# Reordering around TensorE in a hybrid decoder layer: early key and query turns, split head transposes, a later shared expert, and seven half products for the last gate

## What is computed

```
xn  = rms_norm(h);  proj = xn @ w_in
gdn: q,k,v = silu(causal_conv(proj)); q,k = l2_norm; 8 heads of the chunked gated delta rule -> o_a
     y_a = (rms_norm(o_a) * silu(z)) @ w_branch_gdn
fox: q,k = rms_norm per head (16 heads of 64), causal softmax attention with log-forget decay -> y_f
h   = h + (sigmoid(m_a) * y_a + sigmoid(m_f) * y_f) @ w_out
t   = rms_norm(h);  scores = sigmoid(t @ w_router);  top 8 of 64 experts, weights normalised * 2.5
h   = h + sum_e gate_e * (silu(t @ we_gate_e) * (t @ we_up_e)) @ we_down_e + shared expert (same form)
e   = rms_norm(p @ w_ple);  g = sigmoid(rms_norm(h) @ w_ple_gate)
out = h + g * e
```

## Time and profile before

| | us |
|---|---|
| three timed runs, median | 943.53 |
| lowest and highest | 941.88, 945.53 |
| the profiled execution, its own time | 944.93 |
| its span, first to last instruction | 943.2 |
| TensorE busy in it | 917.6 (97%) |
| VectorE busy | 367.3 (39%) |
| ScalarE busy | 190.4 (20%) |
| GpSimd busy | 45.1 (5%) |
| mean granted TensorE clock | 0.995 of full |
| data moved by DMA | 266.00 MB |

### The profile page before, as it was taken

How to read it: one execution, slowest core, us unless ns; L and a number is a source line. 1 busy time by engine, 2 the same in 40 slices (tenths; PEclk the granted TensorE clock), 3 DMA queues, 4 the chain that set the end, 5 groups by cost and what they waited for, 6 DMA issues and landing times.

```text
span 943.2 us, 16601 instructions
## 1 busy us (share of the span) xinstructions
PE 917.6 (97%) x7083; PEld 457.4 (48%) x7083; DVE 367.3 (39%) x789; ACT 190.4 (20%) x383; POOL 45.1 (5%) x72
## 2 busy tenths in 40 slices
PE   6999999999998999999999999999999999999998
PEld 5888655445744554456344344344344344343343
DVE  2556635964585777846121121121121121121132
ACT  1203300012425561132111111111111111111121
POOL 4000202050110000010000000000000000000000
PEclk9999999999999999999999999999999999999999
DMA  7553423662240528683899999999999999999931
GB/s 208 215 179 121 148 90 111 199 197 97 89 172 7 179 90 332 256 348 145 351 418 422 422 422 422 422 422 421 421 422 422 422 422 422 422 422 422 414 119 44
DMA packets 66915, 266.00 MB, mean 282 GB/s; under 512 B 12305, under 2 KB 14722, under 8 KB 41922
## 3 DMA queue, kind: packets, MB, share of 16 engines
q1 hardware_dynamic: 66882, 265.54, 71.3%
HBM read 263.70 MB, written 1.84 MB: 282 GB/s over the span
## 4 chain that ended last, share of the span: by engine, by line
PE 93%; DVE 3%; ACT 2%; issue 1%; DMA 0%; POOL 0%; DVEq 0%; ACTq 0%; POOLq 0%
PE bank L1286 23%; PE bank L890 14%; PE bank L1304 12%; PE bank L990 9%; PE bank L880 9%; PE bank L1268 7%; PE bank L1256 5%; PE bank L1336 3%; PE bank L955 2%; PE bank L1223 1%; PE bank L1293 1%; ACT arena L655 1%; PE bank L867 1%; PE bank L1077 1%; PE bank L1243 1%
## 5 line engine op out<-in xcount | busy, mean ns | idle before, releaser
L1286 PE MATMUL bank<-arena 128*32 128x512 f32 x2048 | 225.6, 592 | 0.9 <-DVE arena L1899 0.9
L1286 PEld LDWEIGHTS bank<-arena 128*32 128x32 f32 x2048 | 66.9, 110 | 153.2 <-issue 152.2
L890 PE MATMUL bank<-arena 128*128 128x512 f32 x264 | 117.7, 598 | 0.0
L1304 PE MATMUL bank<-arena 128*32 128x512 f32 x1024 | 116.5, 595 | 0.0
L1913 DVE SCALAR_TENSOR_TENSOR arena<-arena,gslot,bank 128x256 f32<-128x256 f32 x32 | 15.4, 480 | 211.2 <-ACT arena L837 211.2
L990 PE MATMUL bank<-actT,arena 128*128 128x256 f32 x384 | 86.7, 387 | 1.6 <-DVE actT L1375 1.6
L880 PE MATMUL bank<-arena,actT 128*128 128x512 f32 x192 | 85.3, 603 | 0.3 <-ACT arena L655 0.3
L990 PEld LDWEIGHTS bank<-actT,arena 128*128 128x128 f32 x384 | 73.6, 193 | 12.5 <-issue 1.9
L890 PEld LDWEIGHTS bank<-arena 128*128 128x128 f32 x264 | 49.0, 190 | 58.6 <-issue 58.5
L837 ACT ACTIVATE arena<-bank 128x256 f32<-128x256 f32 x32 | 12.3, 384 | 255.7 <-PE bank L1286 255.7
L1268 PE MATMUL bank<-arena,actT 64*128 64x512 f32 x256 | 63.6, 615 | 0.0
(11 more groups left out here) (275 smaller groups left out, 790.8 us busy)
## 6 DMA issues: line engine op xcount, KB each, us to landing
arena<-in_we_gate SPq DMA_DIRECT2D x32, 2048.0 KB, 18.1
arena<-in_we_up SPq DMA_DIRECT2D x32, 2048.0 KB, 22.6
arena<-in_we_down SPq DMA_DIRECT2D x32, 2048.0 KB, 20.9
arena<-in_w_in SPq DMA_DIRECT2D x17, 2048.0 KB, 7.8
arena<-in_w_branch_gdn SPq DMA_DIRECT2D x2, 2048.0 KB, 7.9
arena<-in_w_branch_fox SPq DMA_DIRECT2D x2, 2048.0 KB, 8.7
arena<-in_w_out SPq DMA_DIRECT2D x2, 2048.0 KB, 9.0
arena<-in_w_ple_gate SPq DMA_DIRECT2D x2, 2048.0 KB, 32.1
```

What stands on the lines that cost most here:

```text
L890: ins = t.matmul(o[:, :], lhs[:, c, :], rhs[:, c, :], start=fresh and c == 0, stop=c == HC - 1, skip_group_check=not fresh)
L1286: ins = t.matmul(bank[4][i * CAP:i * CAP + CAP, :], xg[:, c, i * CAP:i * CAP + CAP], w, start=(c == 0), stop=(c == KC - 1))
L1304: ins = t.matmul(bank[4 + j][i * CAP:i * CAP + CAP, :], hidT[:, c, i * CAP:i * CAP + CAP], d_in[s][:, i % 2, c * D + WT * j:c * D + WT * j ...
```

## The change

Five parts, with no change in what is computed.

- (a) The turns of q and k (`tq.n.0` to `tq.n.3`) move from behind the channel stage into it: one group after each of `qkv.4` to `qkv.11`. ScalarE's copy and square, and VectorE's sum, move along (`turned`, `square_sum`). `qkrinv` is awaited at 8, not 4, before the beta rows.
- (b) The head transposes `fT.0` stand before, `fT.1`, `oT` and `cb.5` to `cb.7` behind the first half product of `m2`; these banks now come from `HEAD_BANKS`. On VectorE `weight_sum(M2_, 2)` goes before `key_decays(5, 6, 7)`.
- (c) In attention's steps 6 and 7 the half product is issued behind the transposes `pT`, before `pv`. VectorE's and ScalarE's order is untouched.
- (d) Shared expert: `sh.0`, `rank`, the gate half of `sh.1`, transposes of 0, up half of `sh.1`, down 0, transposes of 1, gather of pair 0, down 1. VectorE does rank work first and the split of the hidden states into parts (L1851, L1852) after it.
- (e) The tail product becomes seven half products of four matmuls (the seventh as two halves of 256 columns), with the sums on VectorE, two copies on ScalarE and five output blocks in place of four.

```diff
-TQ_ORDER = ((2, 0), (2, 1), (3, 0), (3, 1), (0, 0), (0, 1), (1, 0), (1, 1))
+TQ_ORDER = ((0, 0), (0, 1), (1, 0), (1, 1), (2, 0), (2, 1), (3, 0), (3, 1))
+TQ_BESIDE = {4 + i: f"tq.{n}.{j}" for i, (j, n) in enumerate(TQ_ORDER)}
...
-    f += [f"fT.{n}.{j}" for n in range(NT) for j in range(4)]
-    f += [f"oT.{n}.{j}" for n in range(NT) for j in range(2)]
...
-    g += [(name, HEAD_BANKS) for name in ("cb.5", "cb.6", "cb.7")]
-    g += [("m2.A", PAIR_BANKS), ("m2.C", PAIR_BANKS)]
+    g += [(f"fT.0.{j}", HEAD_BANKS) for j in range(4)] + [("m2.A", PAIR_BANKS)]
...
@@ scalar
             for c in range(12):
+                if c > 3:
+                    turned(c - 4)
                 wait_drained(act, f"qkv.{c}")
...
+            head_columns(0)
+            keep(M2_, 0)
+            head_columns(1)
...
@@ tensor
+                if c2 > 3:
+                    convolved(TQ_BESIDE[c2])
...
                     transposes(f"fT.{n}.{j}", [fox[:, n, P * c:P * c + P] for c in range(4 * j, 4 * j + 4)])
+                if n == 0:
+                    product(M2_, 1)
...
             key_decays(5, 6, 7)
-            product(M2_, 1)
             product(M2_, 5)
...
+            for g in range(8):
+                if g < 6:
+                    fillers(g)
                 for f in (2 * g, 2 * g + 1):
                     pe.wait_ge(sdiv, f + 1)
                     transposes(f"pT.{f}", [scores[f % 4][:, k * P:k * P + P] for k in range(3)])
                 if g < 6:
                     products(g + 2)
+                else:
+                    fillers(g)
                 name = f"pv.{g}"
...
+            open_bank("sh.0")
+            shared(0, sgw, 0)
+            close(shared(0, suw, DE), "sh.0")
...
+            open_bank("sh.1")
+            shared(1, sgw, 0)
+            for b in range(8):
+                if b not in (place["rank"][0], place["sh.1"][0]):
+                    pe.wait_ge(drained[b], opened[b])
+            shared_columns(0)
+            close(shared(1, suw, DE), "sh.1")
+            pe.wait_ge(sdw_loaded, 16)
+            shared_down(0)
+            wait_drained(pe, "sh.1")
+            shared_columns(1)
...
             pe.wait_ge(parts_ready, 2 * NT)
+            wait_drained(pe, "rank")
             gather(1)
+            shared_down(1).then_inc(shared_done, 1)
...
+            pe.wait_ge(hT_ready, 1)
+            gate_product(bank[4][:, :], actT[:, 0:GC, 0:P], gb00)
+            pe.wait_ge(hT_ready, 2)
+            gate_product(bank[5][:, :], actT[:, GC:KC, 0:P], gb10)
+            pe.wait_ge(gtok_made, 1)
+            pe.wait_ge(gdif_made, 1)
+            gate_product(bank[6][:, :], gtok[0], gdif)
+            pe.wait_ge(gtok_made, 3)
+            pe.wait_ge(gdif_made, 2)
+            gate_product(bank[7][:, :], gtok[2], gb00)
+            pe.wait_ge(gtok_made, 4)
+            pe.wait_ge(gkept, 2)
+            gate_product(bank[6][:, :], gtok[3], gb11, False)
+            pe.wait_ge(gdif_made, 3)
+            pe.wait_ge(gjoined, 2)
+            gate_product(bank[7][:, :], gtok[1], gb01, False)
+            pe.wait_ge(gdif_made, 4)
+            pe.wait_ge(hT_ready, 2 * NT)
+            for half in range(2):
+                gate_product(bank[half][:, 0:S], actT[:, GC:KC, P:S], gdif[:, :, half * S:half * S + S])
...
@@ vector
+                if c2 > 3:
+                    square_sum(c2 - 4)
...
-            dve.wait_ge(qkrinv, 4)
+            dve.wait_ge(qkrinv, 8)
...
+            weight_sum(M2_, 2)
             key_decays(5, 6, 7)
-            weight_sum(M2_, 2)
```

More of the change, by code:

```diff
@@ L74, in bank_fills @@
     for c in range(4, 8):
-        f += [f"qkv.{c}", f"gb.{c - 4}"]
-    f += [f"qkv.{c}" for c in range(8, 12)]
-    f += [f"tq.{n}.{j}" for j, n in TQ_ORDER] + ["tq.0.4", "tq.1.4"]
+        f += [f"qkv.{c}", f"gb.{c - 4}", TQ_BESIDE[c]]
+    for c in range(8, 12):
+        f += [f"qkv.{c}", TQ_BESIDE[c]]
+    f += ["tq.0.4", "tq.1.4"]
     for j in range(6):
@@ L110, in bank_fills @@
     f = [f"hT.0.{j}" for j in range(2)] + ["e.0.1", "e.1.0"] + [f"hT.1.{j}" for j in range(2)]
-    f += ["e.1.1", "router"] + [f"sh.{n}" for n in range(NT)] + ["rank"]
+    f += ["e.1.1", "router", "sh.0", "rank", "sh.1"]
     return g + [(name, LAST_BANKS) for name in f]
@@ L548, in _ @@
                 sp.dma_start(wpg[j], w_ple_gate[0].rearrange("(c q) n -> q c n", q=P)[:, :, WT * j:WT * j + WT]).then_inc(wpg_loaded, 16)
[L549 to L553, removed]
+            for i, (n, _, lo, hi) in enumerate(GBLOCKS):
+                sp.wait_ge(out_ready, i + 1)
+                sp.dma_start(out[0, n * P:(n + 1) * P, lo:hi], gt[:, n, lo:hi]).then_inc(out_stored, 16)
+            sp.wait_ge(out_stored, 16 * len(GBLOCKS))
         @block.gpsimd
@@ L746, in _, with head_columns @@
                 activate(M0_, ACT.Sigmoid, n, j)
-            for n in range(NT):
+            def head_columns(n):
                 for j in range(4):
@@ L1013, in _ @@
                     spread_rows(f"gb.{c2 - 4}")
-            for j, n in TQ_ORDER + ((4, 0), (4, 1)):
-                convolved(f"tq.{n}.{j}")
+                if c2 > 3:
+                    convolved(TQ_BESIDE[c2])
+            for n in range(NT):
+                convolved(f"tq.{n}.4")
             for j in range(6):
@@ L1135, in products, with fillers @@
                     close(t.matmul(o[i][:, P:P + S], foxT[hp, g, P:S], foxT[hp, 8 + g, :], start=True, stop=True), f"s.{2 * g + i}")
-            products(0)
-            products(1)
-            for g in range(8):
+            def fillers(g):
                 for p, k in BESIDE_ATTENTION[g]:
@@ L1236, in _, with shared_down @@
                 ins.then_inc(hidT_filled, 1)
-            pe.wait_ge(sdw_loaded, 16)
-            wait_drained(pe, "rank")
-            for n in range(NT):
+            def shared_down(n):
                 pe.wait_ge(hidT_ready, n + 1)
@@ L1889, in _ @@
             place_tokens(slice(0, 2))
+            for n in range(NT):
+                seq(v.tensor_copy(hparts[:, 1, n, :], hn[:, n, :]))
+                v.tensor_tensor(hparts[:, 2, n, :], hn[:, n, :], hparts[:, 1, n, :], ALU.subtract).then_inc(parts_ready, 1)
+            shared_hidden(1)
             wait_drained(dve, "e.1.1")
@@ new lines, in _ @@
+            a00, a01 = actT[:, 0:GC, 0:P], actT[:, GC:KC, 0:P]
+            a10, a11 = actT[:, 0:GC, P:S], actT[:, GC:KC, P:S]
+            dve.wait_ge(added, np_dve * PAIRS + 4)
+            v.tensor_tensor(gtok[0], a10, a11, ALU.add).then_inc(gtok_made, 1)
+            dve.wait_ge(wpg_loaded, 32)
+            v.tensor_tensor(gdif, gb01, gb00, ALU.subtract).then_inc(gdif_made, 1)
+            v.tensor_tensor(gtok[1], a00, a10, ALU.subtract).then_inc(gtok_made, 1)
+            dve.wait_ge(gtok_made, 1)
```

142 lines of the change are left out of this document (89 added, 53 removed).

## The result

| | before | after |
|---|---|---|
| median of five runs, us | 943.53 | 936.23 |
| lowest and highest, us | 941.88, 946.47 | 934.01, 937.85 |
| the profiled execution, its own time | 944.93 | 935.11 |
| its span | 943.2 | 933.4 |

The ratio of the times is 0.9911, 95% interval 0.9894 to 0.9929. The forecast was 936.1.

A forecast was written before the change was run, and what follows sets the result against it. TensorE was taken to bound the kernel; -4.5 - 4.75 + 7.2 - 2.1 - 3.3 = -7.45 us gave 937.5 from the profiled 944.93, or 936.1 for the median, 1.4 lower. Range: 929.5 to 941.5 us.

The forecast's parts named there:

- What bounds the kernel: Whole kernel: TensorE bounds it, 93% of the span, so each part is priced by TensorE's work and waits.
- (a): Channel stage to `fox.0.0`: turns moved into the stage remove waits and low clock; gain 4.5 us, 2.7 if the clock falls.
- the cover: Beta rows: two fox products, 14 us, hide the delay from awaiting `qkrinv` at 8; without them some 2 us lost.
- (b): Head transposes at `m2`: the 3.40 us wait before the decay rows and the low clock go; gain 4.75 us.
- The rival that they let the clock fall: At `m2`: transposes do not hold the clock, second half product at 1.2 GHz; gain there 2.95, time 937.9 us; chance 0.22.
- (c): Attention's steps 6 and 7: TensorE waits for VectorE's scaling, plus one fall of the clock; cost 7.2 us, bounds 5.4 and 9.0.
- the fall of the clock: Attention, behind the second gap, 4.7 us: TensorE's clock falls once, adding 1.8 us.
- (d): Shared expert: reordering covers waits for VectorE, ScalarE and copies; gain 2.1 us, bounds 1.5 and 2.7.
- (e): Tail product: 28 matmuls in place of 32, VectorE's sums ready in time; gain 3.3 us.
- The weight stream: Expert loop: down weights use up the 1.5 us lead, TensorE waits at the last pairs; time 938.2 us; chance 0.08.
- Free attention: Attention: VectorE is further ahead than seen, only the two waits of 0.79 us vanish; time 927.3 us; chance 0.06.
- The slow attention: Attention: clock stays down through its end, steps 6 and 7 cost 19 us; time 947.7 us; chance 0.05.

The follow-up runs named there:

- (d) alone: The kernel before with only the shared expert reordered; median 942.51 us over ten runs, ratio 0.9997.
- the 96 transposes: The changed kernel with attention's steps 6 and 7 put back, plus 96 further transposes in a row ahead of the first `fT` group; 940.13 us, one execution.
- (c) alone: The kernel before with only the half product put behind the `pT` transposes in attention's steps 6 and 7; 952.0 us, ratio 1.0084.
- (b) and (e): Two runs of the kernel before: with only the head transposes split, 940.16 us, ratio 0.9952; with only the tail in half products, 940.91 us, ratio 0.9961.
- the loop with less work: The changed kernel with attention's steps 6 and 7 put back and the second half of each addition of experts' outputs left out; 928.17 us, ratio 0.9824.

## Why the prediction was right, by its steps

**What bounds the kernel.** Right: TensorE is 94% of the chain.

**(a)** -4.8 for -4.5. No wait between the last channel product and the first fox product, 16 records in 7.03 for 8.80: no fall of the clock. In the stage a group of four transposes costs 0.43 us (98.13 to 98.56), so 3.4 for the 32, not 3.7, which is most of the difference. VectorE waits 0.2 us for GpSimd's roots and TensorE does not wait behind that, so the cover was there. In the profile of (d) alone the same product took 7.11 without this part, so the 1.8 us of the fall are not there in every execution.

**(b)** -4.8 for -4.75. No wait of TensorE before the decay rows; the half product between the two groups of transposes takes 3.60, the one behind the second group 3.70. The rival that they let the clock fall is refuted by this and by the 96 transposes.

**(c)** The mechanism was right in each link, the size 1.0 too small. The changed kernel, TensorE then VectorE, in steps 6 and 7 (compare):

```profile
339.99 1.01 PE L887 MATMUL bank<-ident,arena 128*128 128x128 f32 x6 [2.01 <-DVE arena L1755]
340.83 3.60 PE L910 MATMUL bank<-arena 128*128 128x512 f32 x8
...
349.61 1.54 PE L887 MATMUL bank<-ident,arena 128*128 128x128 f32 x6 [4.38 <-DVE arena L1755]
350.94 5.81 PE L910 MATMUL bank<-arena 128*128 128x512 f32 x8
...
357.49 3.70 PE L910 MATMUL bank<-arena 128*128 128x512 f32 x8
```
```profile
344.47 0.69 DVE L1633 TENSOR_TENSOR arena<-arena,bank 128x512 f32<-128x512 f32 x1 [4.08 <-PE bank L910]
...
346.60 2.29 DVE L1605 TENSOR_TENSOR arena<-arena 128x2048 f32<-128x2048 f32 x1
...
349.67 0.35 DVE L1755 TENSOR_SCALAR arena<-arena,dri 128x256 f32<-128x256 f32 x1
```

The join starts as the half product ends (344.43), the 2.29 us weight sum stands behind it, and only then comes the scaling for which TensorE waits. The gaps, forecast at 2.1 and 4.65, were 2.01 and 4.38. The wait for `yf`'s token sum, forecast at 0.35, is listed as 0.18 but cost 0.4 by the starts (24.55 us from `yf`'s first product to its end for 24.14). The mis-sized term is the fall of the clock, taken as 1.8 us from the earlier trace rows. TensorE worked under it from 349.6 to 355.4:

```profile
349.70:351.00 1.30, 1.30 (x7) 1.30 (x8) 0.32 (x2) 0.39 (x1) 0.00 (x0) 0.50 1.06 406
...
355.00:356.00 1.00, 1.00 (x3) 0.47 (x2) 0.00 (x0) 0.00 (x0) 0.00 (x0) 0.81 0.00 0
```

Six transposes took 1.54 for 0.88 and the half product 5.81 for 3.60, so by the starts it cost 2.85. From `pv.5` to the first product of `yf` pass 20.39 us for 12.70, so 7.7 more; without the fall that is 4.85, forecast 5.05. With 1.05 more in the fall, 0.2 less here, and 0.15 in the token sum and ahead of step 6, 7.2 becomes 8.2. In (c) alone the half product behind the same gap took 4.59: one row of a fall is a sample, not a price.

**(d)** -2.5 for -2.1: no wait of TensorE for the pass count in front of the gate product of pair 0, so the 0.86 of the earlier trace rows went whole, not by half. What the prediction had wrong here does not show in this term: it took 14.9 us for the 6 MB of down weights from a steady stretch, ending just before the fourth pair's weights are issued. They were issued 14.8 us behind `sh.0` as forecast, but the last of them landed at 455.0, when the fourth pair's had been issued at 452.15 (before the change, at 457.4 and 457.86). That goes with the loop's lost lead, as above.

**(e)** -3.8 for -3.3. The product's rows have no wait between them:

```profile
904.73 7.03 PE L1374 MATMUL bank<-arena,actT 128*128 128x512 f32 x16
911.60 13.90 PE L1374 MATMUL bank<-arena 128*128 128x512 f32 x32
925.34 3.62 PE L1374 MATMUL bank<-arena,actT 128*128 128x256 f32 x16
```

The product is 3.47 us shorter, so the two halves of 256 columns cost nothing (0.1 forecast, an estimate that no run showed). It begins 0.36 us earlier than the loop's offset says (0.2 forecast). Behind the last matmul 2.3 us pass to the end of the last VectorE operation, 2.65 forecast; before the change these were 2.2 and not the 2.4 that the prediction read.

**Rivals.** The weight stream did not take over in the profiled execution, with 0.2 us to spare. I had put the lead at 1.5, by counting to the weights' expected use; by landing and use it was 1.0. In milder form the rival came true: with (d) in the kernel TensorE waited for weights, 0.5 to 1.2 us as listed and up to 1.7 by the starts, in four of seven profiles with the whole loop. That the changed kernel's profile is among the other three is luck. The chance of 0.08 was low for it. Free attention fell with the first wait. The slow attention did not come: the clock was back before the value product.

**How near.** 936.23 for 936.1 is luck in its last microsecond: the steps were not that close. The parts miss by -0.3, -0.1, +1.0, -0.4 and -0.5, so (c)'s miss is cancelled by the others, and the starts of the two profiled executions differ by 1.8, which five runs of each kernel average out only in part.

## What to carry to other kernels

When a step moves on the engine that bounds, read the other engine's list around what it waits for: where four of VectorE's operations stood decided some 7 us here, and TensorE's order alone put waits of 2.0 and 4.4 us for VectorE in place of two of 0.8 for ScalarE. Measure the parts of a bundle singly: four gains hid a loss nearly as large as the two largest of them together. And when a stage runs on two resources of nearly the same pace, work out by landing and use what lead is left, and ask of each change whether it moves both resources or one. Parts (a) and (b) moved compute and weights together and kept their gain; (d) moved compute against the weights, and is worth only what the lead still covers.

## What the runs showed of the hardware

- A fall of the clock had no fixed price: 1.7 us and 1.8 us, 1.0 and 2.2 us in the half product behind the same gap of 4.4 us, where the clock fell at different moments of the gap. The first fox product behind the waits of the earlier trace rows took 8.80 us in the profiles of before, (b) and (e), and 7.11 in that of (d). No fall came behind the gap of 2.0 us in the three profiles that have it.
- The granted clock does not tell all of the kernel's start: from 12.8 to 28 us it reads 1.00 in profiles where the first two products take 14.05, 15.84 or 17.09 us.
- One core's 16 DMA engines moved 422 GB/s from 460 to 880 us, both before the change and in the loop with less work, where TensorE waited for them. The Trainium skill, "Perfetto Trace Analysis", section Roofline, bounds a core alone by its 16 DMA engines at about 435 GB/s; the trace agrees with 422.
- Of ten executions of (d) alone five took 942.46 to 942.52 us, with mean clocks from 0.993 to 0.996. Why the end does not follow the clock is open.
